# A streaming encoder step on one core: setup's column sums one unit later, the bias table expanded in the feed-forward stage, and norms from column-tiled sums of squares

## The chip, the core and the metric

The kernel runs on one core of a Trainium2 chip. The core has TensorE (PE: matrix products into PSUM), VectorE (DVE), ScalarE (ACT), GpSimd (POOL) and SyncE (SP, which here only issues DMAs); the engines run their own instruction streams and meet at semaphores. The metric is the device time of one execution in microseconds. The kernel before took 3708.29 us, the median of 3 runs (3703.23 to 3716.26).

## The reference

Two layers of a hybrid encoder step for a prompt of 1024 tokens and 8 samples of 16 tokens. Every sub-layer has an adaptive RMSNorm, whose shift, scale and gate come from a conditioning vector, and a gated residual. What the change touches:

```python
def rmsnorm(x, g):
    xf = x.astype(jnp.float32)
    y = xf * lax.rsqrt(jnp.mean(xf * xf, axis=-1, keepdims=True) + RMS_EPS)
    return (y * g.astype(jnp.float32)).astype(x.dtype)

def ada_norm(x, c, w, b, g):
    m = jax.nn.silu(c) @ w + b
    shift, scale, gate = jnp.split(m[:, None, :], 3, axis=-1)
    return rmsnorm(x, g) * (1 + scale) + shift, gate
...
    for l in range(DEPTH):
        # h = ada_norm(x); layer 0: differential and sliding-window attention, layer 1: chunk-band attention
        # x = x + gate * mixer(h);  h = ada_norm(x);  x = x + gate * conv_ffn(h)
...
def relbias_core(q, k, v, table, qpos, kpos, mask):
    rel = jnp.clip(qpos[:, None] - kpos[None, :], -REL_CLIP, REL_CLIP) + REL_CLIP
    s = s + table.astype(jnp.float32)[:, rel][None]
```

## The kernel before

The state x is held transposed, as xT: 8 tiles of 128 features by 1152 tokens (1024 of the prompt, 128 of the samples). The program is a row of blocks with a barrier between them: setup, attention AB (layer 0), feed-forward 0, attention C (layer 1), feed-forward 1, finish. Every f32 product is made of three matmuls (a rounded high part f32r and a bf16 remainder on each side), so weights are split by ScalarE (L183, high) and VectorE (L189, low) after they land.

**Setup.** The modulation of layer 0 is a product of the silu of the conditioning with 24 MB of ada_w, taken in 24 chunks of 1 MB, two to a unit, 12 units. SP loads chunk c into one of four buffers as soon as TensorE has used chunk c - 4 (L274 to L277). TensorE multiplies a chunk in column tiles (`column_tiles`, L211: four matmuls of 32 columns of weights each, side by side in the array). ScalarE copies the unit's result out of PSUM (`m_sums`, L339 to L343), TensorE adds the four strips (`column_sums`, L220), and VectorE adds the bias (`modulation`, L436). TensorE's order is chunk, chunk, column sums, unit by unit; the sums wait for ScalarE's copy. While units 4 and 5 pass, ScalarE and VectorE also do the first norm's modulation (`mod_act`, `mod_dve`, 8 tiles k); the copies of units 4 and 5 stand in ScalarE's order behind tiles k = 4 and k = 6.

SP's queue also carries, after chunk 11, three small stores, and before chunk 17 the expansion of the relative-position table (L286): 16 heads by 128 rows by 256 columns, each row a shifted piece of the reversed table `rev`, from DRAM to DRAM, 2 MB. Behind chunk 21 follows a block of -1e30 into its corner (L290). Attention C reads that table, three stages later.

**The norm at a stage's end.** The last output tile n of a stage is added to xT by VectorE (L2396 in attention, L630 to L633 in feed-forward). ScalarE squares xT[n] (L505), VectorE adds squares in groups (L517), and TensorE sums each group over the features with nine matmuls of one column (L529), giving the sums as 128 tokens by 9. The stages' barrier follows. Then ScalarE takes the root of 128 x 9 (L539), VectorE its reciprocal (L545) and two products with the identity (L573, a diagonal matrix per block of tokens), and TensorE spreads it over all partitions with a matrix of ones (L552, L553). VectorE then scales tile by tile (L589), ScalarE shifts (L559), VectorE takes the remainder (L594), and the first products of the new stage can run.

The feed-forward stage loads weight tiles through a ring of three (raw tiles raws0, raws1 and ffn_raw) in SP's order, each when the tile that it overwrites has been split, and beside them the modulation weights of layer 1 (m_raw, L746).

Of the kernel before, what the change touches and what calls it, by code (L numbers as in the profile page):

```python
# [227 lines left out]
def setup(nc, S, G, ins, ctx):  # L228
# [19 lines left out]
    neg = sb("neg", [CHUNK, CHUNK])  # L248
# [15 lines left out]
    def _(sp):  # L264
# [7 lines left out]
        for c in range(2 * NU):  # L272
# [5 lines left out]
            if c == 11:  # L278
                sp.wait_ge(S.rev_made, 3)
                sp.dma_start(G.rev_dram, rev[:, :]).then_inc(S.rev_out, 16)  # L280
                sp.wait_ge(S.small_evac, 1)
                sp.dma_start(G.whole_dram, whole[:, :, :].rearrange("p k c -> p (k c)")).then_inc(S.small_out, 16)
                sp.dma_start(G.bias_T_dram, bias_T[:, 48:96]).then_inc(S.small_out, 16)
            elif c == 16:
                sp.wait_ge(S.rev_out, 16)
# [201 lines left out]
def group_head(stage, n):  # L487

    return next(g[0] for g in SQ_GROUPS[stage] if n in g)


def added(stage, m, n):

    return SQ_BASE[m] + sum(x != group_head(stage, x) for x in range(n + 1))
# [12 lines left out]


def squares_dve(dve, S, stage, m, sq, n):

    head = group_head(stage, n) if n >= 0 else n
    if head != n:
        into = sq[SQ_AT[stage][head]]
        dve.wait_ge(S.sq_ready, KT * (m - 1) + n + 1)
        if added(stage, m, n) > SQ_BASE[m] + 1:
            dve.wait_ge(S.sq_added, added(stage, m, n) - 1)
        dve.tensor_tensor(into, into, sq[SQ_AT[stage][n]], ALU.add).then_inc(S.sq_added, 1)  # L517


def sums_pe(pe, S, G, stage, m, sq, g):  # L520

    group = SQ_GROUPS[stage][g]
    first, last = g == 0, g == len(SQ_GROUPS[stage]) - 1
    if len(group) > 1:
        pe.wait_ge(S.sq_added, added(stage, m, group[-1]))
    else:
        pe.wait_ge(S.sq_ready, KT * (m - 1) + group[0] + 1)
# [2067 lines left out]
```

## Time and profile before

| | |
|---|---|
| median of 3 runs | 3708.29 us (3703.23 to 3716.26) |
| the profiled execution | 3707.97 us, span 3706.40 us, mean granted clock 0.95 |
| busy: PE / DVE / ACT / POOL | 92% / 55% / 34% / 13% |
| setup | 0 to 112.88 us |
| attention AB | to 967.68 |
| feed-forward 0 | to 1872.30 |
| attention C | to 2817.40 |
| feed-forward 1 | to 3687.73 |
| finish | to 3706.40 |

TensorE is nearly full from the second stage on; what idles is setup and the short time around each border between stages. The chain of waits of this trace reaches back only into the finish stage, so the stages are read from stretches and from the timeline.

### The profile page before, as it was taken

How to read it: one execution, taken by the hardware profiler on the slowest of the kernel's cores; microseconds unless marked ns; L12 is line 12 of the kernel's file. 1: busy time of each engine (PE TensorE's matmuls, PEld its weight loads, DVE VectorE, ACT ScalarE, POOL GpSimd, SP SyncE). 2: the span in 40 equal slices, each digit the busy share in tenths (PEclk: the TensorE clock that was granted, in tenths of full speed). 3: DMA queues.
4: the chain of work that ended last, by engine and by line, in shares of the span. 5: the costliest groups of instructions: out<-in, count | busy, mean ns of one | idle time of the engine just before them, and what ended most of it. 6: DMA issues, size and time to landing. Idle time of an engine off the chain costs nothing. (4 is left out here: it accounts for less than half of the span.)

```text
span 3706.4 us, 54353 instructions
## 1 busy us (share of the span) xinstructions
PE 3398.0 (92%) x20954; PEld 1998.7 (54%) x20954; DVE 2026.8 (55%) x3527; ACT 1246.8 (34%) x2609; POOL 473.5 (13%) x1014
## 2 busy tenths in 40 slices
PE   5889897869899999999988989889898999999998
PEld 2455554536555555555555656556565555555555
DVE  4256655554655554555555555555556555555555
ACT  3254554442322211222244444454423221222221
POOL 1123322221000000000012122222210000000000
PEclk7899999879899999999999999999899999999998
DMA  9423232231223222113133333333521111111111
GB/s 315 120 76 88 86 85 61 58 106 59 65 58 92 63 63 69 57 57 97 47 95 116 110 97 103 111 122 116 190 65 41 41 41 40 46 40 46 39 42 58
DMA packets 247564, 304.14 MB, mean 82 GB/s; under 512 B 24995, under 2 KB 199575, under 8 KB 246754
## 3 DMA queue, kind: packets, MB, share of 16 engines
q1 hardware_dynamic: 217474, 190.70, 16.5%
q0 software_dynamic: 29920, 111.15, 9.9%
q8 instruction: 110, 1.80, 0.2%
q14 instruction: 60, 0.49, 0.0%
HBM read 264.91 MB, written 64.10 MB: 89 GB/s over the span
## 5 line engine op out<-in xcount | busy, mean ns | idle before, releaser
L96 PE MATMUL psum<-h,ffn_high 128*128 128x512 f32 (+1 forms) x2016 | 984.9, 529 | 2.8 <-ACT u L1013 2.8
L98 PE MATMUL psum<-hl,ffn_high 128*128 128x512 bf16 (+1 forms) x2016 | 614.8, 338 | 0.0
L100 PE MATMUL psum<-h,ffn_low 128*128 128x512 bf16 (+1 forms) x2016 | 561.6, 332 | 0.0
L96 PE MATMUL psum<-actr,ffn_high 128*128 128x512 f32 (+1 forms) x960 | 470.1, 530 | 7.3 <-DVE xT L633 7.3
L96 PEld LDWEIGHTS psum<-h,ffn_high 128*128 128x128 f32 x2016 | 389.5, 193 | 88.3 <-issue 8.4
L98 PEld LDWEIGHTS psum<-hl,ffn_high 128*128 128x128 bf16 x2016 | 196.6, 98 | 409.4 <-issue 352.6
L86 PE MATMUL psum<-h,attC_high 128*128 128x384 f32 (+1 forms) x768 | 368.6, 481 | 24.9 <-issue 7.9
L1087 DVE TENSOR_SCALAR y<-u,cvT 128x1168 f32<-128x1168 f32 x88 | 78.2, 888 | 541.4 <-ACT u L1018 541.2
L86 PE MATMUL psum<-h,attAB_high 128*128 128x384 f32 (+2 forms) x672 | 324.0, 483 | 12.7 <-DVE attAB_low L189 5.7
L98 PE MATMUL psum<-actl,ffn_high 128*128 128x512 bf16 (+1 forms) x960 | 294.9, 341 | 0.0
L87 PE MATMUL psum<-hl,attC_high 128*128 128x384 bf16 (+1 forms) x768 | 269.3, 351 | 0.0
L100 PE MATMUL psum<-actr,ffn_low 128*128 128x512 bf16 (+1 forms) x960 | 268.9, 334 | 0.0
L1012 ACT COPY u<-psum 128x1024 f32<-128x1024 f32 x88 | 89.2, 1014 | 527.0 <-PE psum L100 524.6
L88 PE MATMUL psum<-h,attC_low 128*128 128x384 bf16 (+1 forms) x768 | 265.1, 345 | 0.0
L87 PE MATMUL psum<-hl,attAB_high 128*128 128x384 bf16 (+2 forms) x672 | 236.0, 351 | 0.0
L88 PE MATMUL psum<-h,attAB_low 128*128 128x384 bf16 (+2 forms) x672 | 231.5, 345 | 0.0
L633 DVE SCALAR_TENSOR_TENSOR xT<-psum,mod,xT 128x1024 f32<-128x1024 f32 x176 | 224.9, 1278 | 0.0
L822 POOL COPY so<-u 128x2 f32<-128x2 f32 x88 | 17.7, 201 | 1543.5 <-ACT u L1013 1543.5
L96 PEld LDWEIGHTS psum<-actr,ffn_high 128*128 128x128 f32 x960 | 186.7, 195 | 47.8 <-DVE xT L633 13.6
L98 PEld LDWEIGHTS psum<-actl,ffn_high 128*128 128x128 bf16 x960 | 94.2, 98 | 194.1 <-issue 166.7
L86 PEld LDWEIGHTS psum<-h,attC_high 128*128 128x128 f32 x768 | 152.0, 198 | 81.9 <-issue 39.3
L100 PEld LDWEIGHTS psum<-h,ffn_low 128*128 128x128 bf16 x2016 | 173.2, 100 | 0.0
(508 smaller groups left out, 6786.2 us busy)
## 6 DMA issues: line engine op xcount, KB each, us to landing
raws<-in_w_up SPq DMA_DIRECT2D x66, 512.0 KB, 4.0
ada_raw<-in_ada_w SPq DMA_DIRECT2D x24, 1024.0 KB, 9.8
m_raw<-in_ada_w SPq DMA_DIRECT2D x48, 512.0 KB, 7.2
raw_C<-in_cache_c_k POOLq DMA_DIRECT2D x64, 256.0 KB, 4.0
raw_C<-in_cache_c_v POOLq DMA_DIRECT2D x64, 256.0 KB, 3.3
out_ck_s<-in_cache_c_k POOLq DMA_DIRECT2D x8, 1984.0 KB, 8.7
out_cv_s<-in_cache_c_v POOLq DMA_DIRECT2D x8, 1984.0 KB, 13.9
raws<-in_w_in_odd SPq DMA_DIRECT2D x24, 512.0 KB, 4.9
```

The costliest lines, as they stand in the source:

```text
L86: pe.matmul(out, w, x, start=start, stop=False, skip_group_check=True)
L87: pe.matmul(out, top(w), xl, start=False, stop=False, skip_group_check=True)
L88: return pe.matmul(out, wl, top(x), start=False, stop=stop, skip_group_check=True)
L96: return pe.matmul(out, w, x[:, lo:hi], start=first and start, stop=last and stop, skip_group_check=True)
L98: return pe.matmul(out, top(w), xl[:, lo:hi], start=first and start, stop=last and stop, skip_group_check=True)
L100: return pe.matmul(out, wl, top(x[:, lo:hi]), start=first and start, stop=last and stop, skip_group_check=True)
L633: return dve.scalar_tensor_tensor(out=G.xT[:, n, 0:SEQ], in0=y[:, 0:SEQ], scalar=G.mod[:, a, 16 + n, 0:1], in1=G.xT[:, n, 0:SEQ], op0=ALU. ...
L822: pool.tensor_copy(so[:, 2 * g + j, 0:2], U[g][:, SEQ:SEQ + 2])
L1012: act.copy(U[gate][:, 2:2 + SEQ], ps[:, 3 * gate:3 * gate + 2, :].rearrange("p b n -> p (b n)"))
L1087: ch.then(dve.tensor_scalar(y[:, 0:n], u[:, 2:2 + n], cv[:, l, 2, bass.ds(f, 1)], cv[:, l, 3, bass.ds(f, 1)], ALU.mult, ALU.add))
```

## The change

Three things are changed. In setup TensorE takes the column sums of a unit after the chunks of the next unit (those of units 2 and 3 together after unit 3, none after unit 4), ScalarE copies units 4 to 7 after tiles k = 1, 3, 5, 7 and VectorE adds their bias for units 4 and 5 after k = 4 and 6. The expansion of the bias table and its corner go from setup's SP queue into that of feed-forward 0: the first behind its first loads, the second behind its loop. The norm between stages (three of them; the last one, before finish, keeps the old way) is made of four matmuls of 32 columns of ones for each squared tile, each over a quarter of the tokens (288), so that the sums of the four quarters stand in four strips of 32 partitions of one PSUM bank; ScalarE takes the root and VectorE the reciprocal of 128 x 288, and TensorE spreads each quarter with a one-hot column of the identity, in six matmuls cut at the banks' borders. VectorE's additions and diagonal products go. The activation table of the root is loaded ahead of the squares.

```diff
             if c == 11:
-                sp.wait_ge(S.rev_made, 3)
+                sp.wait_ge(S.rev_made, 2)
                 sp.dma_start(G.rev_dram, rev[:, :]).then_inc(S.rev_out, 16)
                 sp.wait_ge(S.small_evac, 1)
...
-            elif c == 16:
-                sp.wait_ge(S.rev_out, 16)
-                sp.dma_start(G.bias_dram, bass.AP(G.rev_dram.tensor, P - 1, [[384, 16], [-1, P], [1, 256]])
-                             ).then_inc(S.rev_out, 16)
-            elif c == 21:
-                sp.wait_ge(S.rev_out, 32)
-                sp.dma_start(G.bias_dram[:, 0:CHUNK, 256 - CHUNK:256].rearrange("h i j -> i h j"),
-                             neg[:, :].unsqueeze(1).broadcast_to([CHUNK, 16, CHUNK])).then_inc(S.rev_out, 16)
         for x in range(2):
             sp.dma_start(rows_by_k(G.raws[x]), first_even(ins, x)).then_inc(S.t_landed[x], 16)
         sp.wait_ge(S.small_out, 32)
-        sp.wait_ge(S.rev_out, 48)
+        sp.wait_ge(S.rev_out, 16)
...
         def between(k):
-            if k in (4, 6):
-                m_sums(4 + (k - 4) // 2)
+            if k % 2:
+                m_sums(4 + k // 2)
 
         mod_act(act, S, G, 0, tmp, ts, between)
-        for u in range(6, NU):
+        for u in range(8, NU):
             m_sums(u)
...
+        def columns(u):
+            pe.wait_ge(S.ada_evac, u + 1)
+            if u >= 2:
+                pe.wait_ge(S.mod_evac, u - 1)
+            column_sums(pe, ps[:, 2 + u % 2, :], m_sum[u % 2], K).then_inc(S.mod_mm, 1)
...
         for u in range(NU):
@@ -397,10 +393,9 @@
             if u == 1:
                 pe.wait_ge(S.x_evac, 2 * TB)
                 spread_pe(pe, S, G, 0, diag, rs, rs_s)
-            pe.wait_ge(S.ada_evac, u + 1)
-            if u >= 2:
-                pe.wait_ge(S.mod_evac, u - 1)
-            column_sums(pe, ps[:, 2 + u % 2, :], m_sum[u % 2], K).then_inc(S.mod_mm, 1)
+            for v in {3: (2, 3), 4: ()}.get(u, (u - 1,) if u else ()):
+                columns(v)
+        columns(NU - 1)
...
         def between(k):
-            if k in (3, 5):
-                modulation(4 + (k - 3) // 2)
+            if k in (4, 6):
+                modulation(4 + (k - 4) // 2)
...
+def squares_act(act, S, G, m, sq, final):
+
+    act.activation(G.root9[:, 0:1], G.ones[:, 0:1], ACT.Sqrt)
+    for n in range(KT):
+        final(n)
+        if n >= 4:
+            act.wait_ge(S.sq_summed, KT * (m - 1) + n - 3)
+        act.activation(sq[n % 4], G.xT[:, n, :], ACT.Square).then_inc(S.sq_ready, 1)
+
+
+def quarters_pe(pe, S, G, m, sq, n, bank):
+
+    pe.wait_ge(S.sq_ready, KT * (m - 1) + n + 1)
+    for j in range(4):
+        mm = pe.matmul(G.psum[32 * j:32 * j + 32, bank, 0:QUARTER], G.ones[:, 0:32],
+                       sq[n % 4][:, j * QUARTER:(j + 1) * QUARTER], start=(n == 0), stop=(n == KT - 1),
+                       skip_group_check=True)
+    mm.then_inc(S.sq_summed, 1)
+
+
+def root_quarters(act, S, G, m, bank, rows):
+
+    act.wait_ge(S.sq_summed, KT * m)
+    act.activation(rows[:, 0:QUARTER], G.psum[:, bank, 0:QUARTER], ACT.Sqrt, scale=1.0 / D,
+                   bias=G.eps[:, 0:1]).then_inc(S.mean, 1)
+
+
+def rstd_quarters(dve, S, G, m, rows):
+
+    dve.wait_ge(S.mean, m + 1)
+    dve.reciprocal(rows[:, QUARTER:2 * QUARTER], rows[:, 0:QUARTER]).then_inc(S.rstd9, 1)
+
+
+def spread_quarters(pe, S, G, m, rows, rs, rs_s):
+
+    pe.wait_ge(S.rstd9, m + 1)
+    for j in range(4):
+        lo, hi = j * QUARTER, (j + 1) * QUARTER
+        row = G.consts[:, C_ID + 32 * j:C_ID + 32 * j + 1].broadcast_to([P, P])
+        for a, b in ((lo, min(hi, 512)), (max(lo, 512), min(hi, SEQ)), (max(lo, SEQ), hi)):
+            if a < b:
+                out = rs[:, a:b] if b <= SEQ else rs_s[:, a - SEQ:b - SEQ]
+                mm = pe.matmul(out, row, rows[:, QUARTER + a - lo:QUARTER + b - lo], start=True, stop=True,
+                               skip_group_check=True)
+    mm.then_inc(S.root, 1)
...
+                if l == 0 and early:
+                    sp.dma_start(G.bias_dram, bass.AP(G.rev_dram.tensor, P - 1, [[384, 16], [-1, P], [1, 256]])
+                                 ).then_inc(S.rev_out, 16)
...
+            if l == 0:
+                sp.wait_ge(S.rev_out, 32)
+                sp.wait_ge(S.rev_made, 3)
+                sp.dma_start(G.bias_dram[:, 0:CHUNK, 256 - CHUNK:256].rearrange("h i j -> i h j"),
+                             neg[:, :].unsqueeze(1).broadcast_to([CHUNK, 16, CHUNK])).then_inc(S.rev_out, 16)
...
+                sp.wait_ge(S.rev_out, 48)
...
+                pool.memset(neg[:, :], NEG).then_inc(S.rev_made, 1)
...
-            spread_pe(pe, S, G, m, Y[0], rs, rs_s)
+            spread_quarters(pe, S, G, m, Y[0], rs, rs_s)
...
-                    if is_last(i) and n == 6:
+                    if l == 0 and is_last(i) and n >= 2:
+                        if n == 2:
+                            pe.wait_ge(S.so_evac, NG)
+                        quarters_pe(pe, S, G, m + 1, sq, n - 2, 6)
+                    if l == 1 and is_last(i) and n == 6:
                         pe.wait_ge(S.st_evac, NG * (l + 1))
-                        if l == 0:
-                            pe.wait_ge(S.mod_evac, NU + NG + 1)
-                        sums_pe(pe, S, G, "ffn", m + 1, sq, 0)
+                        sums_pe(pe, S, G, sq, 0)
...
-            for g in (1, 2):
-                sums_pe(pe, S, G, "ffn", m + 1, sq, g)
+            if l == 0:
+                for n in (KT - 2, KT - 1):
+                    quarters_pe(pe, S, G, m + 1, sq, n, 6)
+            else:
+                for g in (1, 2):
+                    sums_pe(pe, S, G, sq, g)
...
-            root_act(act, S, G, m)
+            root_quarters(act, S, G, m, 7, Y[0])
...
-            squares_act(act, S, G, "ffn", m + 1, sq, final)
+            (squares_by_groups_act if l else squares_act)(act, S, G, m + 1, sq, final)
...
-            rstd_dve(dve, S, G, m)
-            diag_dve(dve, S, G, m, Y[0])
+            rstd_quarters(dve, S, G, m, Y[0])
...
-                    if isinstance(i, int) and i == NG - 1:
-                        squares_dve(dve, S, "ffn", m + 1, sq, n - 1)
-                        if l == 0 and n == 4:
-                            mod_evac(NG)
+                    if l == 1 and isinstance(i, int) and i == NG - 1:
+                        squares_dve(dve, S, m + 1, sq, n - 1)
+                    if l == 0 and isinstance(i, int) and i == NG - 1 and n == 4:
+                        mod_evac(NG)
...
-                if n in (4, 6):
-                    sums_pe(pe, S, G, "att", m + 1, sq, n // 2 - 2)
-            for g in (2, 3):
-                sums_pe(pe, S, G, "att", m + 1, sq, g)
+                if n >= 3:
+                    quarters_pe(pe, S, G, m + 1, sq, n - 3, 7)
+            for n in range(KT - 3, KT):
+                quarters_pe(pe, S, G, m + 1, sq, n, 7)
...
-                root_act(act, S, G, m)
+                root_quarters(act, S, G, m, 6, F["v"])
...
-            squares_act(act, S, G, "att", m + 1, sq, final)
+            squares_act(act, S, G, m + 1, sq, final)
...
-                rstd_dve(dve, S, G, m)
-                diag_dve(dve, S, G, m, F["v"])
+                rstd_quarters(dve, S, G, m, F["v"])
...
-                squares_dve(dve, S, "att", m + 1, sq, n - 1)
-            squares_dve(dve, S, "att", m + 1, sq, KT - 1)
```

TensorE in setup, before: units 3 to 5, where L215 are the chunks (ada_raw) and L223 the column sums (m_sums0 and m_sums1 alternate by unit).

```order
L215 MATMUL psum<-ada_raw2,c_whole 32x512 x4
L215 MATMUL psum<-ada_raw3,c_whole 32x512 x4
L223 MATMUL psum<-consts,m_sums1 128x10 x4
L215 MATMUL psum<-ada_raw0,c_whole 32x512 x4
L215 MATMUL psum<-ada_raw1,c_whole 32x512 x4
L223 MATMUL psum<-consts,m_sums0 128x10 x4
L215 MATMUL psum<-ada_raw2,c_whole 32x512 x4
L215 MATMUL psum<-ada_raw3,c_whole 32x512 x4
L223 MATMUL psum<-consts,m_sums1 128x10 x4
```

The same place in the changed kernel, from unit 3 on.

```order
L215 MATMUL psum<-ada_raw2,c_whole 32x512 x4
L215 MATMUL psum<-ada_raw3,c_whole 32x512 x4
L223 MATMUL psum<-consts,m_sums0 128x10 x4
L223 MATMUL psum<-consts,m_sums1 128x10 x4
L215 MATMUL psum<-ada_raw0,c_whole 32x512 x4
L215 MATMUL psum<-ada_raw1,c_whole 32x512 x4
L215 MATMUL psum<-ada_raw2,c_whole 32x512 x4
L215 MATMUL psum<-ada_raw3,c_whole 32x512 x4
L223 MATMUL psum<-consts,m_sums0 128x10 x4
L215 MATMUL psum<-ada_raw0,c_whole 32x512 x4
L215 MATMUL psum<-ada_raw1,c_whole 32x512 x4
L223 MATMUL psum<-consts,m_sums1 128x10 x4
```

The sums of unit 4 (m_sums0) now stand behind all chunks of unit 5.

TensorE from the last output tile of attention AB into feed-forward 0, before: L86 to L88 are products, L529 the sums of a group, L552 and L553 the spreading.

```order
L86 MATMUL psum<-h,attAB_high0 128x512
L87 MATMUL psum<-hl,attAB_high0 128x512
L88 MATMUL psum<-h,attAB_low0 128x512
L529 MATMUL psum<-ones,f_k_AB 128x1 x9
L529 MATMUL psum<-ones,sw_AB 128x1 x9
L1308 UNCONDITIONAL_BRANCH
L841 UNCONDITIONAL_BRANCH
L552 MATMUL psum<-y0_0,ones 128x512 x2
L553 MATMUL psum<-y0_0,ones 128x128
L86 MATMUL psum<-h,ffn0_high0 128x512
```

The same place in the changed kernel: L506 are the quarter sums of a tile, L534 the spreading.

```order
L88 MATMUL psum<-h,attAB_low0 128x512
L506 MATMUL psum<-f_q_AB,ones 32x288 x4
L506 MATMUL psum<-f_k_AB,ones 32x288 x4
L506 MATMUL psum<-f_v_AB,ones 32x288 x4
L506 MATMUL psum<-E_AB,ones 32x288 x4
L1364 UNCONDITIONAL_BRANCH
L891 UNCONDITIONAL_BRANCH
L534 MATMUL psum<-y0_0,consts 128x288
L534 MATMUL psum<-y0_0,consts 128x224
L534 MATMUL psum<-y0_0,consts 128x64
L534 MATMUL psum<-y0_0,consts 128x288
L534 MATMUL psum<-y0_0,consts 128x160
```

Four sets stand behind the last product now (four more are strewn ahead of it, one behind each of tiles 3 to 6), and a sixth piece of 128 columns ends the spreading.

## Rows read from the trace of the kernel before

**Rows 1.** Busy time by stretches: span, us and instructions by engine, clock, DMA share, GB/s; setup.

```profile
0.00:112.88 112.88, 66.51 (x380) 32.30 (x380) 43.79 (x72) 32.56 (x45) 9.91 (x28) 0.75 0.88 302
```

**Rows 2.** Busy time by stretches, as above, three stretches of setup.

```profile
25.00:50.00 25.00, 18.69 (x116) 7.75 (x116) 9.27 (x28) 6.43 (x10) 0.00 (x0) 0.88 1.05 387
...
60.00:65.00 5.00, 3.51 (x16) 2.18 (x20) 4.93 (x6) 2.59 (x3) 0.00 (x0) 0.50 0.00 0
...
85.00:90.00 5.00, 0.00 (x0) 0.00 (x0) 0.00 (x0) 0.00 (x0) 0.00 (x0) 0.50 1.05 389
```

**Rows 3.** Timeline of setup: start, us, engine, line, idle before and its releaser.

```profile
25.91 1.07 PE L215 MATMUL psum<-ada_raw,c_whole 128*32 128x512 f32 x8 [1.47 <-DMA ada_raw<-in_ada_w]
...
47.99 0.20 PEld L215 LDWEIGHTS psum<-ada_raw,c_whole 128*32 128x32 f32 x8 [1.87 <-DMA ada_raw<-in_ada_w]
...
61.49 1.88 PE L223 MATMUL psum<-consts,m_sums 128*128 128x10 f32 x8 [11.56 <-ACT m_sums L343]
...
90.26 1.94 PE L215 MATMUL psum<-ada_raw,c_whole 128*32 128x512 f32 x8 [8.90 <-DMA ada_raw<-in_ada_w]
...
107.84 1.93 PE L215 MATMUL psum<-ada_raw,c_whole 128*32 128x512 f32 x8 [1.44 <-DMA ada_raw<-in_ada_w]
...
110.47 1.88 PE L223 MATMUL psum<-consts,m_sums 128*128 128x10 f32 x8 [0.70 <-ACT m_sums L343]
...
112.89 1.99 ACT L183 CAST attAB_high<-raws 128x1024 fp32r<-128x1024 f32 x2 [2.47 <-PEq L2555]
```

**Rows 4.** DMA issues of setup: count, KB each, median us from issue to landing.

```profile
ada_raw<-in_ada_w SPq DMA_DIRECT2D x24, 1024.0 KB, 9.8
...
bias_dram<-rev_dram SPq DMA_DIRECT2D x1, 2048.0 KB, 17.2
```

**Rows 5.** Timeline of the border from attention AB to feed-forward 0.

```profile
955.89 2.06 PE L529 MATMUL psum<-ones,f_v_AB 128*128 128x1 f32 x18
...
960.79 1.16 ACT L505 ACTIVATE E_AB<-xT 128x1152 f32<-128x1152 f32 x1 [2.21 <-DVE xT L2396]
...
961.99 1.36 DVE L517 TENSOR_TENSOR sw_AB<-sw_AB,E_AB 128x1152 f32<-128x1152 f32 x1 [1.23 <-ACT E_AB L505]
...
963.40 4.00 PE L529 MATMUL psum<-ones,sw_AB 128*128 128x1 f32 x18 [2.06 <-DVE sw_AB L517]
...
967.70 0.27 ACT L539 ACTIVATE root<-psum,columns 128x9 f32<-128x9 f32 x1 [4.23 <-PEq L1308]
...
968.25 1.43 DVE L573 TENSOR_TENSOR y<-consts,rstd 128x512 f32<-128x512 f32 x2
...
969.00 3.55 PE L552 MATMUL psum<-y,ones 128*128 128x512 f32 x4 [1.60 <-DVE y L573]
...
972.81 2.47 DVE L589 SCALAR_TENSOR_TENSOR u<-xT,gs,psum 128x1024 f32<-128x1024 f32 x2 [0.86 <-PE psum L553]
```

**Rows 6.** Timeline of the two later borders: last square, first scaled tile.

```profile
1865.41 1.16 ACT L505 ACTIVATE y<-xT 128x1152 f32<-128x1152 f32 x1 [3.99 <-DVE xT L633]
...
1877.38 1.28 DVE L589 SCALAR_TENSOR_TENSOR f_q_C<-xT,gs,psum 128x1024 f32<-128x1024 f32 x1 [0.81 <-PE psum L553]
...
2811.58 1.16 ACT L505 ACTIVATE E_C<-xT 128x1152 f32<-128x1152 f32 x1 [2.22 <-DVE xT L2396]
...
2822.68 2.47 DVE L589 SCALAR_TENSOR_TENSOR u<-xT,gs,psum 128x1024 f32<-128x1024 f32 x2 [1.00 <-PE psum L553]
```

**Rows 7.** Timeline of TensorE in feed-forward 0: two column-tiled sets in a row.

```profile
1033.52 1.92 PE L215 MATMUL psum<-m_raw,whole 128*32 128x512 f32 x16
```

**Rows 8.** Groups by line and form, VectorE's reciprocals: busy us, mean ns, idle before.

```profile
L2344 DVE RECIPROCAL st_C<-st_C 128x2 f32<-128x2 f32 x64 | 10.5, 163 | 1.5
...
L545 DVE RECIPROCAL rstd<-root 128x9 f32<-128x9 f32 x5 | 1.1, 215 | 19.8 <-ACT root L539 19.8
```

**Rows 9.** Timeline of the start of feed-forward 0: a weight load's issue and its split.

```profile
977.92 0.41 SPq L172 DMA_DIRECT2D raws<-in_w_up  x1
...
1010.29 1.08 ACT L183 CAST ffn_high<-raws 128x1024 fp32r<-128x1024 f32 x1
```

More of the change, by code:

```diff
@@ L247, in setup @@
     rev = sb("rev", [16, 384])
-    neg = sb("neg", [CHUNK, CHUNK])
     maskf = sb("maskf", [NB, C_N - C_L])
@@ L477, in _ @@
                 scales(1)
-SQ_GROUPS = {"att": ((0, 1), (2, 3), (4, 5), (6, 7)), "ffn": ((0, 1, 2, 3), (4, 5), (6, 7))}
-SQ_AT = {"att": (0, 1, 2, 3, 1, 3, 4, 3), "ffn": (0, 1, 2, 3, 1, 2, 3, 2)}
-SQ_BASE = (None, 0, 4, 9, 13)
+SQ_GROUPS = ((0, 1, 2, 3), (4, 5), (6, 7))
+SQ_AT = (0, 1, 2, 3, 1, 2, 3, 2)
+QUARTER = TOK // 4
 LAG = 4
[L487 to L494, printed above, removed]
@@ L497, in squares_act, with group_head, added @@
-def squares_act(act, S, G, stage, m, sq, final):
-    at = SQ_AT[stage]
+def group_head(n):
+    return next(g[0] for g in SQ_GROUPS if n in g)
+def added(n):
+    return sum(x != group_head(x) for x in range(n + 1))
+def squares_act(act, S, G, m, sq, final):
[5 more added lines that the diff above has]
+        act.activation(sq[n % 4], G.xT[:, n, :], ACT.Square).then_inc(S.sq_ready, 1)
@@ L500, in squares_act, with squares_by_groups_act @@
+def squares_by_groups_act(act, S, G, m, sq, final):
+    at = SQ_AT
+    act.activation(G.root9[:, 0:1], G.ones[:, 0:1], ACT.Sqrt)
     for n in range(KT):
@@ L503, in squares_act, with squares_dve, sums_pe @@
         if held:
-            act.wait_ge(S.sq_added, added(stage, m, held[-1]))
+            act.wait_ge(S.sq_added, added(held[-1]))
         act.activation(sq[at[n]], G.xT[:, n, :], ACT.Square).then_inc(S.sq_ready, 1)
-    act.activation(G.root9[:, 0:1], G.ones[:, 0:1], ACT.Sqrt)
-def squares_dve(dve, S, stage, m, sq, n):
-    head = group_head(stage, n) if n >= 0 else n
+def squares_dve(dve, S, m, sq, n):
+    head = group_head(n) if n >= 0 else n
     if head != n:
-        into = sq[SQ_AT[stage][head]]
+        into = sq[SQ_AT[head]]
         dve.wait_ge(S.sq_ready, KT * (m - 1) + n + 1)
[L515 to L527, printed above, removed]
+        if added(n) > 1:
+            dve.wait_ge(S.sq_added, added(n) - 1)
+        dve.tensor_tensor(into, into, sq[SQ_AT[n]], ALU.add).then_inc(S.sq_added, 1)
+def sums_pe(pe, S, G, sq, g):
+    group = SQ_GROUPS[g]
+    first, last = g == 0, g == len(SQ_GROUPS) - 1
+    pe.wait_ge(S.sq_added, added(group[-1]))
     for t in range(TB):
-        mm = pe.matmul(G.psum[:, 7, t:t + 1], sq[SQ_AT[stage][group[0]]][:, t * P:(t + 1) * P], G.ones[:, 0:1],
+        mm = pe.matmul(G.psum[:, 7, t:t + 1], sq[SQ_AT[group[0]]][:, t * P:(t + 1) * P], G.ones[:, 0:1],
                        start=(first and t == 0), stop=(last and t == TB - 1), skip_group_check=True)
@@ L535, in root_act @@
 def root_act(act, S, G, m):
-    act.wait_ge(S.sums, m + 1)
+    act.wait_ge(S.sums, 2 if m else 1)
     src = G.psum[:, 7, 0:TB] if m else G.square_sums[:, :]
@@ L1164, in _ @@
             down_evac(NG - 1, fb + FCH - 2, 0, 0, KT)
-            squares_dve(dve, S, "ffn", m + 1, sq, KT - 1)
+            if l == 1:
+                squares_dve(dve, S, m + 1, sq, KT - 1)
 FFN_DVE_STEPS = 16
@@ L1725, in _ @@
             if odd:
-                spread_pe(pe, S, G, m, F["v"], rs, rs_s)
+                spread_quarters(pe, S, G, m, F["v"], rs, rs_s)
             def do(what, kind, T, s, c, turns):
@@ L2476, in __init__ @@
             "mod_mm mod_evac set_step")
-        (self.sq_ready, self.sq_added, self.root, self.hs_ready, self.hs_high, self.hs_low, self.hp_ready, self.hp_high) = make(
-            "sq_ready sq_added root hs_ready hs_high hs_low hp_ready hp_high")
+        (self.sq_ready, self.sq_added, self.sq_summed, self.root, self.hs_ready, self.hs_high, self.hs_low, self.hp_ready, self.hp_high) = make(
+            "sq_ready sq_added sq_summed root hs_ready hs_high hs_low hp_ready hp_high")
         (self.hp_low, self.sums, self.mean, self.rstd9, self.diag) = make(
```

2 lines of the change are left out of this document (1 added, 1 removed).

## The prediction

> **What bounds the kernel now.** I read the busy time by stretches first. Setup is the one stage in which TensorE is far from full: 66.5 of 112.88 us at a mean granted clock of 0.75 [rows 1]. The reader should then see that three things hold it in turn. From 25 to 50 us the DMA engines are full at 387 GB/s. From 60 to 65 us they move nothing. From 85 to 90 us they are full again at 389 GB/s, while no compute engine does anything [rows 2].
>
> The timeline says why. While the DMA leads, the weight chunks of 1 MB come evenly: chunk 1 is used at 25.91 us, chunk 9 at 47.99 us, so (47.99 - 25.91)/8 = 2.76 us a chunk. Then TensorE sits idle for 11.56 us before the column sums of unit 4, released by ScalarE's copy of m_sums [rows 3]: that copy stands behind the modulation of tile k = 4, TensorE waits for it before it takes chunk 10, and with four buffers held no load is issued. That is the empty DMA window. Chunk 17 brings the second stop: TensorE waits 8.90 us for it, to 90.26 us [rows 3]. In the SP queue it stands directly behind the expansion of the bias table, 2 MB from DRAM to DRAM, which took 17.2 us to land against 9.8 us for a 1 MB chunk [rows 4]. Chunk 23 is used at 107.84 us, its sums run to 110.47 + 1.88, and the next stage starts at 112.89 us [rows 3].
>
> The other places are the borders between stages. After the last square of the first attention stage (960.79 + 1.16 = 961.95) comes a chain of single steps: VectorE's addition 1.36, TensorE's sums 4.00 (the clock has fallen: the same nine matmuls took 2.06 a moment earlier), root 0.27, two diagonal products 1.43, the spreading from 969.00 on, and the first scaled tile at 972.81: 10.86 us [rows 5]. The two later borders take 1877.38 - 1866.57 = 10.81 and 2822.68 - 2812.74 = 9.94 us [rows 6].
>
> **Setup, step by step.** The column sums of a unit now come after the next unit's chunks, so TensorE no longer stands before a copy that waits for the modulation, and ScalarE copies units 4 to 7 after tiles 1, 3, 5 and 7 instead of units 4 and 5 after tiles 4 and 6. The expansion is out of the queue. What is late next is the DMA itself. Carrying its pace on, chunk 23 is there at 47.99 + 14 x 2.76 = 86.6 us. Units arrive every 5.5 us. TensorE's work on one is two chunks at 1.07 and sums, and at half clock 2 x 1.94 + 1.88 = 5.8 [rows 3], so it keeps up at either clock, with 2 us of lag that the four buffers absorb. The modulation doesn't set the end: even before, VectorE and ScalarE were done with it by 85 us [rows 2], and in the new order each copy stands behind chunks that have come by then. After chunk 23: 1.93 for the chunk, 1.88 for the sums of unit 10 (they hide ScalarE's copy of unit 11), 1.88 for unit 11, and 0.54 to the next stage (112.89 - 112.35): 92.8 us. The gain is 112.89 - 92.8 = **20.1 us**. The first attention weights, 1 MB behind chunk 23, land within this. Bounds: 10 us if only the stop at chunk 17 goes, 22.5 if the last steps run at full clock.
>
> **The expansion in the feed-forward stage.** It is issued after the first m_raw loads and ahead of the weight load that was issued at 977.92 us. ScalarE takes that tile at 1010.29 us [rows 9], 32 us later; even 17.2 us for the expansion leaves it early. The small DMA of the masked corner and the wait for the expansion stand near the end of the stage, hundreds of microseconds behind it. I take 0. If the cover were gone, each microsecond past 1010 would cost one.
>
> **The norms.** Removed are the additions, the diagonal products and the nine one-column matmuls a group at three borders; the last norm keeps them. New is a set of four matmuls of 32 rows and 288 columns for each of eight tiles. Column-tiled sets are in the trace: one set with 512 columns takes 1.07 us (8 pieces) [rows 3], two in a row 1.92 (16 pieces) [rows 7]. So a second set adds 0.85 and 0.22 is fixed: 0.85 x 288/512 + 0.22 = 0.70 us a set at full clock.
>
> The Trainium skill ("TensorEngine Tiling (Array Packing)", Tiling Modes) says that changing the tiling mode drains TensorE, which speaks against sets strewn among full-array matmuls. The 0.22 us of these rows is what such a change could cost here: without it the sets ahead of the last products and in the chains (5, 6 and 5) would save another 3.5 us.
>
> Ahead of the last product matmul, which TensorE's order delays: at an attention stage four sets (2.8) replace two groups (2 x 2.06 [rows 5]), -1.3 us. In the first feed-forward stage five sets (3.5) replace one group, +1.4. The additions on VectorE hide under TensorE there.
>
> The chain after the last square then is: set 0.70; to the next stage's root 0.30 (967.40 to 967.70 [rows 5]); root of 288 columns 0.27 + 279 x 0.78 ns = 0.49 (the slope from the 9-column root and the 1152-column square [rows 5]); reciprocal; spreading; some 0.15 of hand-overs. The reciprocal of 288 columns is the unknown. Two columns take 0.163 us and nine 0.215 [rows 8], 7.4 ns a column, so 0.163 + 286 x 7.4 ns = 2.28. The lower bound is the rate of an ordinary operation (1.36 us for 1152 columns [rows 5]): 0.5 us. I take 2.28, since the rows of the operation itself say so.
>
> The Trainium skill ("VectorE: DVE perf modes", Walkthrough: the 8-slice pipeline in each mode) says that the reciprocal is an iterative divide with a repeat count of 8. By it my estimate is eight cycles a column, 2.4 us rather than 2.28, and three borders 0.4 us dearer; at one cycle a column they would be 5.3 us cheaper.
>
> The spreading keeps 1152 columns of f32, in six matmuls instead of three; before 969.00 to 972.81 = 3.8 [rows 5], now 4.0. At full clock it would be 2.0, but TensorE idles some 3 us ahead of it, and after 2.06 us of idling it ran at the slow pace [rows 5]. Sum: 0.70 + 0.30 + 0.49 + 2.28 + 4.0 + 0.15 = 7.9 us.
>
> Borders: 10.86 - 7.9 + 1.3 = 4.3; 10.81 - 7.9 - 1.4 = 1.5; 9.94 - 7.9 + 1.3 = 3.3. Together **9.1 us**. The root's table load, now ahead of the squares, lay beside other work before (0). The last border keeps its chain (0).
>
> **Sum.** The profiled execution took 3707.97 us (span 3706.40 and 1.57 around it), the median of the runs is 3708.29, so no shift. 3707.97 - 20.1 - 9.1 = 3678.8, **3679 us**.
>
> **Rivals.**
> - Setup gains only the stop at chunk 17. For it: ScalarE still copies between modulation tiles, in order, and each stop there empties the four buffers again, as the 11.56 us did. Against: every copy now belongs to a unit whose chunks came some 5 us before. Gain 10 instead of 20: 3689 us.
> - The borders are cheaper: the reciprocal at an ordinary rate (-5.3), the spreading at full clock (-1.8 to -2.0 each), or both: 3668 to 3674. For the clock: the sets keep TensorE busy up to the chain. Against: the slope of the reciprocal [rows 8] and the 4.00 us that the sums took after a short idle [rows 5].
> - The four matmuls of a set run one after the other, about 0.48 each, 1.92 a set. Attention borders: 4 x 1.92 - 4.12 = +3.6 ahead and a chain of 9.1; feed-forward +7.5 ahead. The borders then lose 10 instead of gaining 9: 3698, not told from no change. Against: one set of 512 columns took 1.07 in all.
> - Slower: the expansion collides with the feed-forward weights. The load behind it has to land after 1010 us before anything is lost, and each microsecond more costs one; to eat 29 us and 11 more it would have to land near 1050 us, some 72 us after its issue. In setup the expansion landed in 17.2 us under full load. From 1050 on the kernel is slower: 3720 us or more.
>
> **Chances.** Forecast 0.67, half a setup gain 0.14, cheaper borders 0.10, serial sets 0.04, collision 0.03, and 0.02 for what I don't see. About 0.3% (11 us) is what a measurement of this kernel tells from no change. Faster: the first three, 0.91. Same: serial sets and the unseen, 0.06. Slower: 0.03. The range, 3667 to 3692, reaches over the half setup gain and most of the cheap borders.
>
> **What would show it.** In setup: chunks used every 2.76 us through 60 us and 85 us, no DMA window at 0, next stage at 91 to 94 us. At each border: a reciprocal of about 2.3 us with 288 columns, sets of 0.6 to 0.8 us, from the last square to the first scaled tile near 8 us. In the feed-forward stage: ScalarE's cast of the third raws tile not waiting for a DMA. Wrong if TensorE waits for ScalarE's m_sums by more than 2 us in setup, if the reciprocal is under 1 us, or if the spreading takes 2 us.

## The result and the profile after

The changed kernel took 3673.1 us (median of 4 runs, 3666.62 to 3678.22) against 3706.05 us before: ratio 0.990, 95% interval 0.9882 to 0.9918. Two later repeats, on two chips, gave 0.9914 (0.9890 to 0.9937) and 0.9911 (0.9889 to 0.9932). It is faster by some 33 us. The forecast was 3679, 29 us less than before.

The profiled execution took 3666.62 us (span 3664.6), 41 us less than that of before. That is more than the medians differ by, and the stages show where the surplus lies.

Setup, busy time by stretches (span, us and instructions of PE, PEld, DVE, ACT, POOL, then granted clock, DMA share, GB/s):

```profile
0.00:93.95 93.95, 68.33 (x380) 31.39 (x380) 44.91 (x74) 34.34 (x47) 11.59 (x31) 0.79 0.97 341
25.00:50.00 25.00, 19.50 (x116) 7.92 (x116) 9.85 (x28) 7.36 (x12) 0.00 (x0) 0.82 1.04 378
60.00:65.00 5.00, 3.85 (x24) 1.32 (x24) 4.93 (x5) 2.00 (x3) 0.00 (x0) 0.83 1.05 387
85.00:90.00 5.00, 5.00 (x27) 1.64 (x26) 0.43 (x2) 0.59 (x1) 0.00 (x0) 0.60 0.92 241
```

The window from 60 to 65 us, in which the DMA moved nothing [rows 2], now runs at 387 GB/s, and from 85 to 90 us TensorE is busy throughout. TensorE's timeline in setup (start, us, line, idle before and its releaser), and ScalarE's first split of the next stage:

```profile
48.05 1.93 PE L215 MATMUL psum<-ada_raw,c_whole 128*32 128x512 f32 x8 [1.65 <-DMA ada_raw<-in_ada_w]
...
56.09 1.88 PE L223 MATMUL psum<-consts,m_sums 128*128 128x10 f32 x8
...
85.38 3.80 PE L215 MATMUL psum<-ada_raw,c_whole 128*32 128x512 f32 x16
89.12 1.95 PE L223 MATMUL psum<-consts,m_sums 128*128 128x10 f32 x16
```

```profile
91.59 1.99 ACT L183 CAST attAB_high<-raws 128x1024 fp32r<-128x1024 f32 x2 [1.75 <-PEq L2608]
```

No column sum waits for ScalarE any more and no chunk waits longer than 1.65 us: TensorE follows the DMA. The next stage starts at 91.59 us instead of 112.89 [rows 3], 21.3 us earlier.

The border from attention AB into feed-forward 0, three engines in turn, where [rows 5] has the old steps:

```profile
938.46 0.69 PE L506 MATMUL psum<-f_q_AB,ones 128*32 128x288 f32 x8
938.97 0.67 PE L506 MATMUL psum<-f_k_AB,ones 128*32 128x288 f32 x8
939.45 0.67 PE L506 MATMUL psum<-f_v_AB,ones 128*32 128x288 f32 x8
941.10 0.69 PE L506 MATMUL psum<-E_AB,ones 128*32 128x288 f32 x8 [0.98 <-ACT E_AB L499]
944.66 3.42 PE L534 MATMUL psum<-y,consts 128*128 128x288 f32 x12 [2.87 <-DVE y L522]
```

```profile
939.88 1.16 ACT L499 ACTIVATE E_AB<-xT 128x1152 f32<-128x1152 f32 x1 [1.04 <-DVE xT L2451]
942.12 0.50 ACT L515 ACTIVATE y<-psum,columns 128x288 f32<-128x288 f32 x1 [1.08 <-PEq L1364]
```

```profile
942.65 1.95 DVE L522 RECIPROCAL y<-y 128x288 f32<-128x288 f32 x1 [2.81 <-ACT y L515]
...
948.12 2.47 DVE L628 SCALAR_TENSOR_TENSOR u<-xT,gs,psum 128x1024 f32<-128x1024 f32 x2 [1.30 <-PE psum L534]
```

From the last square's end (941.04) to the first scaled tile, the chain of this border, is 7.08 us, where it was 10.86. A set takes 0.69 us alone, and the next ones of a row start 0.51 and 0.48 us apart. The later borders, squares on ScalarE and scaled tiles on VectorE, answer to [rows 6]:

```profile
1844.38 1.16 ACT L499 ACTIVATE y<-xT 128x1152 f32<-128x1152 f32 x1 [2.79 <-DVE xT L672]
...
2773.19 1.16 ACT L499 ACTIVATE E_C<-xT 128x1152 f32<-128x1152 f32 x1 [1.04 <-DVE xT L2451]
```

```profile
1853.62 1.28 DVE L628 SCALAR_TENSOR_TENSOR f_q_C<-xT,gs,psum 128x1024 f32<-128x1024 f32 x1 [2.31 <-PE psum L534]
...
2781.77 2.47 DVE L628 SCALAR_TENSOR_TENSOR u<-xT,gs,psum 128x1024 f32<-128x1024 f32 x2 [1.64 <-PE psum L534]
```

8.08 us instead of 10.81, and 7.42 instead of 9.94. Ahead of the last square, the time from VectorE's third to its eighth tile of the output goes from 11.19 to 10.21 us (AB), 18.61 to 20.60 (feed-forward 0) and 11.17 to 10.17 (C). So the borders give 4.8, 0.7 and 3.5 us, 9.0 in all.

The expansion of the bias table, now in feed-forward 0 (issue to landing, us), and ScalarE's split of the weight tile behind it:

```profile
bias_dram<-rev_dram SPq DMA_DIRECT2D x1, 2048.0 KB, 12.9
```

```profile
985.61 1.08 ACT L183 CAST ffn_high<-raws 128x1024 fp32r<-128x1024 f32 x1
```

21.3 and 9.0 are 30.3 of the 41. The rest comes from the middle of attention C. Busy time from root to root (ScalarE's root at one border to that at the next), before and after:

```profile
1872.32:2817.43 945.11, 849.93 (x5710) 556.63 (x5710) 526.09 (x1126) 423.04 (x919) 188.72 (x348) 0.95 0.35 111
```

```profile
1846.62:2775.43 928.81, 824.11 (x5708) 535.96 (x5708) 521.11 (x1120) 423.32 (x918) 188.72 (x348) 0.97 0.36 113
```

C is 16.3 us shorter, of which its entry (+1.9, root to scaled tile) and its end (-4.6) explain 2.7. The count of matmuls is nearly the same and the clock is 0.97 instead of 0.95. The 13.6 us left are more than was missing, because the middles of attention AB and feed-forward 0 are 1.4 and 1.7 us longer than their steps say.

### The profile page after: what moved, and what is told of

Its sections match the earlier page's. It is cut to its first block and busy times, and to the rows that moved or that the text cites. A ratio compares the mean times of both kernels' runs of the same rounds, so it can differ in the third digit from the quotient of the medians.

```text
span 3664.6 us, 54348 instructions
## 1 busy us (share of the span) xinstructions
PE 3364.6 (92%) x20966; PEld 1962.4 (54%) x20966; DVE 2010.5 (55%) x3508; ACT 1247.3 (34%) x2609; POOL 475.3 (13%) x1014
## 5 line engine op out<-in xcount | busy, mean ns | idle before, releaser
L86 PE MATMUL psum<-h,attC_high 128*128 128x384 f32 (+1 forms) x768 | 361.3, 471 | 31.2 <-DMA hl<-act_low_dram 10.6
L86 PE MATMUL psum<-h,attAB_high 128*128 128x384 f32 (+2 forms) x672 | 323.9, 483 | 13.0 <-DVE attAB_low L189 5.7
L88 PE MATMUL psum<-h,attC_low 128*128 128x384 bf16 (+1 forms) x768 | 259.8, 338 | 0.0
L88 PE MATMUL psum<-h,attAB_low 128*128 128x384 bf16 (+2 forms) x672 | 231.9, 345 | 0.0
L96 PEld LDWEIGHTS psum<-actr,ffn_high 128*128 128x128 f32 x960 | 186.4, 194 | 47.6 <-DVE xT L672 13.6
L86 PEld LDWEIGHTS psum<-h,attC_high 128*128 128x128 f32 x768 | 148.7, 194 | 88.4 <-issue 44.4
```

The lines of the kernel that those rows point to most:

```text
L86: pe.matmul(out, w, x, start=start, stop=False, skip_group_check=True)
L88: return pe.matmul(out, wl, top(x), start=False, stop=stop, skip_group_check=True)
L96: return pe.matmul(out, w, x[:, lo:hi], start=first and start, stop=last and stop, skip_group_check=True)
```

## The experiments

All times of a kind are put together. The experiments come from three series on two chips, in which the kernel before has means of 3710.3, 3707.6 and 3706.8 us. In all, 71 runs of the kernel before have a mean of 3708.6 us with a standard deviation of 7.8, and 16 of the changed kernel a mean of 3675.0. With such spread only means over many runs part a few microseconds; "±" below is one standard error.

**The parts apart.** The first four kernels are the kernel before with some hunks of the diff (shortened here): the setup order alone (the column sums, ScalarE's and VectorE's steps between tiles), the expansion alone, both, and the norms alone.

```diff
 order_only, setup_both:  + for v in {3: (2, 3), 4: ()}.get(u, (u - 1,) if u else ()): columns(v)
 bias_only, setup_both:   - elif c == 16: ... bias_dram   + if l == 0 and early: ... bias_dram
 norms_only:              - sums_pe, diag_dve, spread_pe  + quarters_pe, rstd_quarters, spread_quarters
```

> The kernel before with the new setup order alone; the expansion of the bias table stays in setup's queue, the norms stay. Theory (two stops that add up): the stop before the sums of unit 4 goes, and DMA leads from 25 us on; the expansion still holds the queue for 2 MB read and 2 MB written, at 389 GB/s 10.8 us. Chunk 23 at 86.6 + 10.8 = 97.4, next stage at 97.4 + 6.2 = 103.6 us instead of 112.9: gain 9 us, about 3697. Rival (the stops hide each other): setup ends where the last DMA lands, and the expansion uses up what the order gave: no gain, next stage at 112 to 113 us. Stage C about 945 us long as before if its 16 us shorter time in the changed kernel belongs to the norms or to the moved expansion; anything from 929 to 945 if that was chance.

The mean was 3699.5 ± 3.0 (ratio 0.9978, 0.9955 to 1.0002). TensorE and ScalarE of this kernel in setup:

```profile
80.22 1.94 PE L215 MATMUL psum<-ada_raw,c_whole 128*32 128x512 f32 x8 [9.45 <-DMA ada_raw<-in_ada_w]
```

```profile
103.46 1.99 ACT L183 CAST attAB_high<-raws 128x1024 fp32r<-128x1024 f32 x2 [3.40 <-PEq L2560]
```

The stop at chunk 17 stays (9.45 us, the expansion lands in 16.5) and the next stage starts at 103.46: 9.4 us gained. The rival that expected none falls.

> The kernel before with the expansion of the bias table moved to feed-forward 0 alone. Theory (two stops that add up): the stop before the sums of unit 4 stays and costs what is left of the measured 18.9 us; next stage at 101 to 104 us, gain 9 to 11 us, about 3696. Feed-forward 0 not longer by more than 1 us. Rival (collision in feed-forward 0): that stage is longer by 2 us or more. Rival (stops hide each other): gain near 19 or near 0. Stage C shorter here if the 16 us belong to the moved expansion.

Mean 3695.5 ± 2.5 (0.9968, 0.9947 to 0.9988). The other stop is the one that stays:

```profile
60.80 1.88 PE L223 MATMUL psum<-consts,m_sums 128*128 128x10 f32 x8 [10.40 <-ACT m_sums L333]
```

```profile
101.35 1.99 ACT L183 CAST attAB_high<-raws 128x1024 fp32r<-128x1024 f32 x2 [2.46 <-PEq L2556]
```

Gain in setup 11.5 us. 9.4 and 11.5 make 20.9 of the 21.3: two separate stops that add up. Feed-forward 0 took 904.66 us from root to root against 904.62 before, so no cost of the expansion shows there (over all profiles that stage takes 901.9 to 906.3 us, with and without it).

> The kernel before with both setup parts and the old norms. Theory: next stage at 93.9 us as in the changed kernel, gain 19 us, about 3687; border chains 10.9, 10.8 and 9.9 us as before. Stage C about 945 us if the norms made it 16 us shorter (they explain 3 of it), near 929 if the setup parts did, anything between if it was chance.

Mean 3688.8 ± 2.5 (0.9943, 0.9918 to 0.9967), next stage at 93.18 us: 19.7 us gained. (The 93.9 and 18.9 us of these expectations set the changed kernel's first product, 93.95, against the old first split, 112.89; split against split it is 21.3.) One pair of profiles tells this gain to some 3 us only: the old setup ends between 110.1 and 112.9 us in five profiles, the new one between 91.2 and 93.5 in seven, and the means are 19.3 apart. C took 942.5 us here, 931.0 with the order alone and 935.3 with the expansion alone. Neither part set C's length; with one and the same code it goes over 14 us.

> The kernel before with the new norms alone; setup as before (next stage at 113 us). Theory: chains from the last square to the first scaled tile 7.1, 8.1 and 7.4 us, attention AB 6 us shorter from its start to its root, feed-forward stages as before, C 3 us shorter: gain 9 us, about 3697. Rival (the norms also make C faster by keeping TensorE's clock up): C near 929 us, gain 22 us, about 3684.

Mean 3693.0 ± 1.8 (0.9952, 0.9932 to 0.9972): 15.6 us less than before, where the steps read from the trace give 9.0. C took 933.8 us, between the two theories. The mean granted clock of its runs was 0.9551 against 0.9499.

**Which border?** In the next two, the new norm stands at some borders only (`NEW` holds their numbers, and every count of a semaphore follows it).

```diff
+NEW = (2,)     # norm_into_c;  (1, 3) in norm_into_ffn
-            spread_pe(pe, S, G, m, Y[0], rs, rs_s)
+            (spread_quarters if m in NEW else spread_pe)(pe, S, G, m, Y[0], rs, rs_s)
```

> The kernel before with the new norm at one border only, from feed-forward 0 into attention C. The three norms together gained 17 us by the means of the runs (3710.3 to 3693.0) where their chains and the sums ahead explain 9. Theory 1 (each border is worth its own steps): chain 8.1 instead of 10.8 us, five sets ahead for one group, +1.4: gain 1 to 2 us, mean about 3709, mean granted clock as before, 0.950. Rival (the entry of C decides how often its clock falls in mid-stage): gain 8 to 10 us, mean about 3701, granted clock 0.953 or more.

Mean 3701.2 ± 1.8 (0.9980, 0.9967 to 0.9994), granted clock 0.9536. Against the kernel before in its own series the mean is 6.4 ± 2.5 us lower.

> The kernel before with the new norm at the two borders into the feed-forward stages, and the old one into attention C. Theory 1: chains 7.1 and 7.4 instead of 10.9 and 9.9 us and 1.3 us ahead of each: gain 7 to 9 us, mean about 3702. Rival (the entry of C decides how often its clock falls): the same 7 to 9 us, and what is missing to 17 shows in the other kernel. Second rival (the ends of the attention stages carry more than the chain, since the clock no longer falls there): gain 14 to 16 us, mean about 3695, granted clock 0.954.

Mean 3703.7 ± 3.2 (0.9984, 0.9961 to 1.0006), clock 0.9503, chains 7.67 and 7.61 us: 4.9 ± 3.3 us less than before, not the second rival's 14 to 16. A least-squares fit over the 181 runs, with a constant for each part, gives: setup -20.0 ± 1.8, the norms into the feed-forward stages -5.7 ± 1.8 (the trace's steps: -8.3), the norm into C -8.2 ± 1.8 (its steps: -0.7). So by the runs it is the entry into C that gives more than its steps, and with it the mean granted clock of the whole execution rises by 0.0038 ± 0.0007. In the 71 runs of before 0.001 of it goes with 2.3 us (correlation -0.89): that is about the missing amount.

> The changed kernel once more, with more runs and a second profile. If stage C's 928.8 us were of the change, C is 927 to 931 us again; if it was chance of the clock, C may lie anywhere from 925 to 942, and the times spread over 25 to 35 us with the granted clock (2.3 us per 0.001). Gain over before by the means 31 us if norms are worth what the chains say and setup 21, 37 to 39 if the means of the two parts alone add up.

Mean 3677.6 over 6 runs, C 929.0 us. The mean is 29.9 ± 4.8 us below the kernel before in its series, which doesn't decide between 31 and 37. The length of C spoke for a fixed pattern; the third profile did not.

> The changed kernel for comparison on the same chip: mean 3670 to 3680 us. Theory A: C has one long stretch at the low clock at 149 us again and takes 929 us. Theory B: any number, C 925 to 942 us.

Mean 3673.9 ± 2.2. C from root to root in this profile of the same kernel:

```profile
1845.99:2785.91 939.92, 842.70 (x5708) 547.05 (x5708) 521.14 (x1120) 423.64 (x919) 189.09 (x348) 0.95 0.35 111
```

By windows of 2 us there are four stretches of about 13.6 us at half clock between 100 and 755 us of the stage; the two other profiles have one there. The 11 us between the profiles for three stretches more make some 3.6 us for each. The third profile is of another chip, but there halves_ffn (below), with the same entry into C, took 928.9 us. So what C takes differs from execution to execution, and one profile of a kernel does not tell its clock. Over all profiles, C has 2 to 5 such stretches with the old entry (five profiles, mean 3.4) and 1 to 4 with the new one (nine, mean 2.0), which points the same way as the fit and is no proof by itself. How little decides it shows in the kernel before, at two passes of one loop, windows of 2 us and TensorE's waits in them:

```profile
2014.00:2016.00 2.00, 0.95 (x7) 0.56 (x7) 1.25 (x4) 0.68 (x2) 1.52 (x3) 1.00 0.03 3
2016.00:2018.00 2.00, 0.88 (x7) 0.39 (x5) 1.50 (x3) 1.67 (x3) 1.96 (x4) 1.00 0.17 31
2018.00:2020.00 2.00, 2.00 (x22) 1.63 (x22) 1.52 (x2) 1.07 (x2) 0.00 (x0) 1.00 1.45 513
2112.00:2114.00 2.00, 1.24 (x8) 0.80 (x8) 1.87 (x4) 0.44 (x1) 2.00 (x4) 1.00 0.09 15
2114.00:2116.00 2.00, 0.88 (x11) 0.84 (x10) 1.11 (x2) 1.69 (x3) 1.23 (x3) 0.91 1.42 468
2116.00:2118.00 2.00, 2.00 (x13) 1.32 (x12) 1.71 (x2) 0.62 (x1) 0.00 (x0) 0.50 0.16 63
```

```profile
2015.53 0.77 PE L1829 MATMUL psum<-consts,E_C 128*128 128x128 f32 x5 [1.05 <-DVE E_C L2360]
2017.93 0.33 PE L86 MATMUL psum<-W_C,v_C 128*128 128x128 f32 x1 [1.12 <-DVE Wl_C L2226]
...
2112.76 0.77 PE L1829 MATMUL psum<-consts,E_C 128*128 128x128 f32 x5 [1.05 <-DVE E_C L2360]
2115.17 0.33 PE L86 MATMUL psum<-W_C,v_C 128*128 128x128 f32 x1 [1.12 <-DVE Wl_C L2226]
```

The same two waits of 1.05 and 1.12 us, and the same work of TensorE in the 10 us ahead of them; after the first pair the clock stays at 1.00, after the second it falls to 0.50 (1.2 GHz).

**Is it when C is entered?** norm_into_c with its reciprocal taken twice there:

```diff
+    dve.reciprocal(rows[:, 2 * QUARTER:3 * QUARTER], rows[:, 0:QUARTER])
     dve.reciprocal(rows[:, QUARTER:2 * QUARTER], rows[:, 0:QUARTER]).then_inc(S.rstd9, 1)
```

> The kernel with the new norm into attention C alone, and its reciprocal taken twice there (the first into columns that nothing reads), so that C's first products come about 2 us later than in that kernel, near where they come with the old norm. In the profiles so far C entered through the old norm had 2 to 5 stretches of about 13.6 us at the low clock between 100 and 755 us of the stage, and entered through the new one 1 or 2. Theory A (it is when C is entered, against the pattern of its own work): the mean goes back to 3708 to 3711 us, 3 or more such stretches, first at 242 us of the stage. Theory B (it is what the norm does): mean 3703 us (3701 and the 2 us of the added work), 1 or 2 such stretches, first at 150 us. Chain 10.0 us in both.

Mean 3703.7 ± 2.7, chain 9.9 us, C 934.9 us with one long stretch at the low clock, first at 149 us. Pattern and mean are those of theory B. But the mean is only 1.6 standard errors below theory A's 3708, and the kernel before had 3706.8 in the same series (ratio 0.9994, 0.9976 to 1.0013): the times can't tell the two theories apart. Single profiles had proved to tell little, so the pattern leans against A without closing it.

**TensorE kept busy ahead of the spreading.** warm puts matmuls into the wait for the reciprocal at all three borders, warm_c into C's alone, halves_ffn three of them at the two others with the reciprocal in halves.

```diff
 def spread_quarters(pe, S, G, m, rows, rs, rs_s):
+    for x in range(5):
+        pe.matmul(rs[:, 0:256], G.ones[:, :], G.xT[:, x, 0:256], start=True, stop=True, skip_group_check=True)
     pe.wait_ge(S.rstd9, m + 1)
 halves_ffn:
+    dve.reciprocal(rows[:, QUARTER:QUARTER + h], rows[:, 0:h]).then_inc(S.half, 1)
+    dve.reciprocal(rows[:, QUARTER + h:2 * QUARTER], rows[:, h:QUARTER]).then_inc(S.rstd9, 1)
```

> The changed kernel with five matmuls of 256 columns put on TensorE while it waits for the reciprocal at each border (results overwritten by the spreading). Theory (the spreading is slow because the clock fell in the idle time): it takes 2.0 to 2.3 instead of 3.4, 4.4 and 3.8 us, the chains get 1.2 to 2.3 us shorter, 4 to 5 us in all over the changed kernel. Rival (the clock is down already when the wait begins): the five take 4.4 us instead of 2.2, the spreading starts up to 1.9 us later and is no faster: 3 to 6 us lost.

TensorE in warm at the first two borders:

```profile
941.79 2.40 PE L528 MATMUL psum<-xT,ones 128*128 128x256 f32 x10 [0.35 <-PEq L1366]
944.31 2.33 PE L536 MATMUL psum<-y,consts 128*128 128x288 f32 x12
...
1843.65 4.06 PE L528 MATMUL psum<-xT,ones 128*128 128x256 f32 x10 [0.35 <-PEq L708]
1847.51 2.29 PE L536 MATMUL psum<-f_v_C,consts 128*128 128x288 f32 x12
```

The spreading and the granted clock (the figure after the instruction counts) at the same borders of the changed kernel:

```profile
1849.16 4.42 PE L534 MATMUL psum<-f_v_C,consts 128*128 128x288 f32 x12 [2.87 <-DVE f_v_C L522]
...
2777.98 3.76 PE L534 MATMUL psum<-y,consts 128*128 128x288 f32 x12 [2.88 <-DVE y L522]
```

```profile
944.00:946.00 2.00, 1.34 (x7) 1.23 (x8) 2.00 (x3) 0.50 (x1) 0.00 (x0) 0.94 0.91 245
946.00:948.00 2.00, 2.00 (x7) 1.50 (x6) 0.82 (x1) 0.00 (x0) 0.00 (x0) 0.50 0.13 36
...
1846.00:1848.00 2.00, 0.29 (x8) 0.00 (x0) 0.84 (x1) 1.38 (x3) 1.39 (x3) 0.71 0.00 0
1848.00:1850.00 2.00, 0.84 (x2) 0.69 (x3) 2.00 (x2) 1.00 (x2) 1.22 (x3) 0.50 0.02 4
```

The spreading falls from 3.42, 4.42 and 3.76 to 2.33, 2.29 and 2.33 us: the slow clock behind the wait was its cost, as the theory has it. But only into C had the clock fallen in the wait itself. At the first border it was 1.00 until 944 us and 0.94 over the next two, so it fell some 1.1 us after the spreading had begun (some 0.7 us at the third border). Into C the rival is right too: there a wait of 1.99 us stands ahead of the last set, the five ran slowly (4.06 us) and held the spreading up, and only then was the clock back. Chains 5.99, 7.29 and 6.00, together 3.3 us shorter. The mean, 3674.7 ± 3.8, can't show that: C took 943.9 us in the profile.

> The changed kernel with the five matmuls ahead of the spreading at the border into attention C alone: chain 7.3 instead of 8.1 us. In the kernel that had them at all borders C took 943.9 us with four long stretches at the low clock from 246 us on, against 929 with one at 149 us in both profiles of the changed kernel. Theory A (when C is entered): four such stretches again, C 940 us or more, mean 5 to 10 us above the changed kernel. Theory B (that profile was chance): mean 1 us below the changed kernel, C's stretches as often as there.

Mean 3678.6 ± 2.2, 3.6 ± 2.9 above the changed kernel; C 933.3 us with two long stretches. Between the theories: inconclusive.

> The changed kernel with three matmuls ahead of the spreading, and the reciprocal in two halves of 144 columns, so that the spreading of the first halves runs beside the second reciprocal; at the borders into the feed-forward stages alone. Chains there 5.0 to 5.4 us instead of 7.1 and 7.4 (1.1 from the clock as measured, 0.9 from the halves): 4 us less than the changed kernel, mean 3671 if that is 3675. If ten smaller pieces cost more than the overlap gives, the chains stay at 5.9 to 6.2 us.

Mean 3672.6 ± 1.3, 2.4 ± 2.3 below the changed kernel, not told apart from it. TensorE and VectorE at the first border:

```profile
951.25 2.63 PE L538 MATMUL psum<-y,consts 128*128 128x144 f32 x20
```

```profile
950.14 1.05 DVE L547 RECIPROCAL y<-y 128x144 f32<-128x144 f32 x1 [2.81 <-ACT y L515]
951.11 0.99 DVE L548 RECIPROCAL y<-y 128x144 f32<-128x144 f32 x1
952.02 1.16 DVE L646 TENSOR_TENSOR y<-xT,gs 128x1024 f32<-128x1024 f32 x1
953.10 1.21 DVE L189 TENSOR_TENSOR ffn_low<-raws,ffn_high 128x1024 bf16<-128x1024 f32 x1
954.23 2.46 DVE L654 SCALAR_TENSOR_TENSOR u<-xT,gs,psum 128x1024 f32<-128x1024 f32 x2
```

The chain is 5.70 us at both borders. Of the 0.9 us hoped for, 0.3 came. The spreading begins beside the second half and its ten pieces take 2.63 instead of 2.33 us, but they end at 953.88 and don't set the end: the first scaled tile starts at 954.23 with no idle time before it, right behind VectorE's own two operations (L646 and the weight split L189). In warm VectorE still waited 0.22 us for the spreading there, so little more was to be had from TensorE; the order on VectorE is what limits this chain now. No kernel here is measurably faster than the changed one.

## Why the prediction was right, and where it was not

- **Setup, -20.1.** 21.3 in the trace, 20.0 ± 1.8 in the runs. The mechanism is shown by its halves. The rival "half a setup gain", in which only the stop at chunk 17 goes, is what bias_only is (11.5 us gained); the other half, order_only, ended at 103.46 us, where its expectation worked from the same rows said 103.6.
- **The expansion, 0.** It landed in 12.9 us in feed-forward 0, and ScalarE splits the tile behind it 43.5 us after the root (985.61 - 942.12) against 42.6 before [rows 9], with no wait for a DMA: the 0.9 us are the new norm's longer way from the root. The collision didn't happen.
- **The sets, 0.70.** 0.69, and 0.48 to 0.51 for those that follow one another, as 0.85 x 288/512 had it. They do run side by side. Ahead of the last square they moved -1.0, +2.0 and -1.0 us (forecast -1.3, +1.4, -1.3). The sets strewn among products carry a fixed 0.2 us. The Trainium skill ("TensorEngine Tiling (Array Packing)", Tiling Modes) says that a change of the tiling mode drains TensorE. No run here tells that from another fixed cost: the last set, which starts after 0.98 us of idle time, takes 0.69 us too.
- **The reciprocal, 2.28.** 1.95 us. From 9 to 288 columns that is (1.953 - 0.216)/279 = 6.2 ns a column, so the bound of 0.5 is out. The Trainium skill ("VectorE: DVE Perf Modes", Walkthrough: the 8-slice pipeline in each mode) gives the reciprocal a repeat count of 8. Read as eight cycles a column, that was an estimate of 2.4 us, too dear by a fifth, but on the right side.
- **The spreading, 4.0.** 3.42, 4.42 and 3.76, and 2.3 with TensorE kept busy (the forecast said 2.0 at full clock). The slow clock after the wait was the right reason, though at two of the three borders it fell only when the spreading had begun.
- **The borders, 4.3, 1.5 and 3.3.** 4.8, 0.7 and 3.5 by the trace: 9.0 against 9.1. That the sum agrees so well is partly luck: the errors of +0.5, -0.8 and +0.2 us at the three borders cancel.
- **The term that was mis-sized** is the border into C. Its steps are worth 0.7 us (forecast 1.5), but the runs with it are 8.2 ± 1.8 us shorter. The forecast counted steps at the border only, and took the clock in the stages' long middle as given. This is large enough to account for the 4 to 6 us by which the time came out below the forecast. Why C keeps its clock more often when it is entered this way is open: the moment of entry was tried, and one profile speaks against it where the times can't decide; nothing else of the norm was tried.

## What to carry to other kernels

A stall that leaves the DMA idle and a transfer that stands ahead of the one needed add up when one queue paces both: count the queue's time, not the engines'. Divide a border into single steps and price each from the nearest row; here each came out within 1.3 us. And before a difference between two profiles is explained, look whether the same kernel shows it against itself: here C differed by 11 us between two profiles of one kernel.

## What was not expected of the hardware

The same pair of waits (1.05 and 1.12 us, in one execution) left TensorE's clock at 1.00 at one pass and brought it to 0.50 at the next. The times of one kernel spread over 45 us (3684 to 3729, 71 runs), and they follow the mean granted clock (correlation -0.89). And a matmul can be worth its place for the clock alone: 2.4 us of work whose result nobody reads made the 3.4 us after it 1.1 us shorter.
